# Zeroed matrix products added between the warm-up and the first real product of a decoder trunk

## The reference, cut to what matters

```python
h = rms_norm(x, norm_mix[l])
proj = h @ w_in[l]                       # 2048 x 5120
q, k, v, hq, hf, hi, hg, cb, cc, ch = jnp.split(proj, split_idx, axis=-1)
a = swa_prompt(...)  # or swa_sample: windowed attention with sinks
o, S_new = hgrn2_mixer(hq, hf, hi, hg, S0, lower_bound[l], hgrn_norm[l])
yc, buf_new = short_conv(cc * ch, buf, conv_w[l])
x = x + jnp.concatenate([a, o, cb * yc], axis=-1) @ w_out[l]
h = rms_norm(x, norm_ffn[l])
gate, up = jnp.split(h @ w_gate_up[l], 2, axis=-1)
x = x + (jax.nn.silu(gate) * up) @ w_down[l]
```

## Time and profile before

| | |
|---|---|
| median of the two runs | 2547.41 us (2547.26 to 2547.55) |
| profiled execution | 2545.56 us |
| its span, first to last instruction | 2544.0 us |
| TensorE busy | 2530.7 us, 19426 matrix instructions |
| VectorE, ScalarE, GpSimd busy | 1475.7, 1016.2, 330.8 us |
| first warm-up pass, first real product (starts) | 1.74 and 9.79 us |

### The profile page before, as it was taken

The page is one execution under the profiler, slowest core; times in us unless marked ns, Lnnn a source line. Parts: engine busy times, 40 slices in busy tenths (PEclk is TensorE's granted clock), DMA queues, the critical chain, the costliest instruction groups (busy, mean ns, idle before and its releaser), DMA issues.

```text
span 2544.0 us, 51052 instructions
## 1 busy us (share of the span) xinstructions
PE 2530.7 (99%) x19426; PEld 2503.1 (98%) x19426; DVE 1475.7 (58%) x2011; ACT 1016.2 (40%) x1412; POOL 330.8 (13%) x279
## 2 busy tenths in 40 slices
PE   9999999999999999999999999999999999999998
PEld 9999999999999999999999999999999999999998
DVE  6678787555554445555545787775555444555544
ACT  5454554333333333333334545443333333333333
POOL 3011003111110011111100200131111000111111
PEclk9999999999999999999999999999999999999999
DMA  6545445454455444454455554454444554544553
GB/s 233 173 159 182 158 143 170 157 165 165 165 171 168 157 165 165 165 165 166 165 166 166 177 174 153 142 166 166 165 165 165 165 168 163 165 165 165 166 166 136
DMA packets 116516, 420.84 MB, mean 165 GB/s; under 512 B 13840, under 2 KB 15120, under 8 KB 116368
## 3 DMA queue, kind: packets, MB, share of 16 engines
q1 hardware_dynamic: 109296, 397.72, 47.2%
q0 software_dynamic: 4112, 14.78, 1.8%
q10 hardware_dynamic: 3024, 7.16, 0.9%
HBM read 411.06 MB, written 11.87 MB: 166 GB/s over the span
## 4 chain that ended last, share of the span: by engine, by line
PE 97%; DVE 1%; ACT 1%; issue 0%; DVEq 0%; POOL 0%; POOLq 0%
PE gp L1601 31%; PE gp L1605 31%; PE gp L1603 31%; PE mb L1654 1%; PE mb L1765 0%; PE mb L1778 0%; PE mb L1847 0%; PE mb L1786 0%; PE mb L1663 0%; ACT sc L564 0%; PE mb L1712 0%; PE mb L1729 0%; ACT sc L562 0%; DVE wlo L767 0%; PE mb L1840 0%
## 5 line engine op out<-in xcount | busy, mean ns | idle before, releaser
L767 DVE TENSOR_TENSOR wlo<-raw,whi 128x1024 fp32r<-128x1024 f32 x754 | 987.0, 1343 | 362.7 <-ACT whi L427 359.3
L427 ACT ACTIVATE whi<-raw 128x1024 fp32r<-128x1024 f32 x754 | 768.7, 1051 | 583.6 <-PE gp L1605 549.5
L1601 PE MATMUL gp<-xh,whi 128*128 128x288 f32 x4096 | 885.7, 297 | 0.0
L1605 PE MATMUL gp<-xl,whi 128*128 128x288 f32 x4096 | 877.0, 295 | 0.0
L1603 PE MATMUL gp<-xh,wlo 128*128 128x288 f32 x4096 | 875.0, 295 | 0.0
L1601 PEld LDWEIGHTS gp<-xh,whi 128*128 128x128 f32 x4096 | 656.5, 188 | 7.7 <-issue 5.9
L1603 PEld LDWEIGHTS gp<-xh,wlo 128*128 128x128 f32 x4096 | 659.2, 188 | 0.0
L1605 PEld LDWEIGHTS gp<-xl,whi 128*128 128x128 f32 x4096 | 655.7, 188 | 0.0
L1605 PE MATMUL gp<-fl,whi 128*128 128x288 f32 x1408 | 303.2, 296 | 0.0
L1603 PE MATMUL gp<-fh,wlo 128*128 128x288 f32 x1408 | 301.1, 295 | 0.0
L1601 PE MATMUL gp<-fh,whi 128*128 128x288 f32 x1408 | 301.0, 294 | 0.0
(11 more groups left out here) (266 smaller groups left out, 1656.2 us busy)
## 6 DMA issues: line engine op xcount, KB each, us to landing
raw<-wstream SPq DMA_DIRECT2D x754, 512.0 KB, 4.3
s<-s_cache POOLq DMA_DIRECT2D x8, 512.0 KB, 10.6
hs_out<-s ACTq DMA_DIRECT2D x8, 512.0 KB, 3.3
caches_out<-caches POOLq DMA_DIRECT2D x8, 496.0 KB, 8.7
x<-x_in ACTq DMA_DIRECT2D x4, 576.0 KB, 8.6
kct<-kt_cache POOLq DMA_DIRECT2D x4, 512.0 KB, 6.1
vct<-v_cache POOLq DMA_DIRECT2D x4, 512.0 KB, 6.8
y_out<-x SPq DMA_DIRECT2D x3, 576.0 KB, 2.9
```

Of the source, the lines that this page charges most:

```text
L427: a.activation(whi[slot][:], raw[slot][:], ACT.Copy).then_inc(hi_ready, 1)
L767: v.tensor_tensor(wlo[slot][:], raw[slot][:], whi[slot][:].bitcast(F32), ALU.subtract).then_inc(lo_ready, 1)
L1601: t.matmul(outs[c], whi[slot][:, k, c * P:(c + 1) * P], mv_hi, start=first, stop=False)
L1605: mm = t.matmul(outs[c], whi[slot][:, k, c * P:(c + 1) * P], mv_lo, start=False, stop=end)
```

## The change

GpSimd's list of memsets becomes two longer: `zero_w`, 384 numbers per partition, and `zero_m`, 4096 numbers per partition, both zero, of type fp32r, both starting on a multiple of 512 bytes in `wide`. The waits for `ones_set` on ScalarE, VectorE and TensorE go from 5 to 7. Behind the warm-up TensorE does 22 series. A series is one product of `mean_x` with itself into `mb[1]`, and then a list of rounded products of 128 x 128 zeroed weights and 288 zeroed columns, all added up in `mb[0]`. Each product of the list names the byte at which its weights begin in `zero_w` and the byte at which its columns begin in `zero_m`.

- 11 series of ten products with the same two offsets: 0, 32, 64, 128 or 256 bytes for the one, the other or both.
- 5 series of ten in which the columns alternate between offset 0 and 1152, 1280, 1536, 8192 or 8320 bytes.
- 3 series of 24 that step through four rows of 1152, 1280 or 1536 bytes, with three products a row: the row itself, one 8192 bytes on, and the first again with weights 512 bytes on.
- 3 series of 24 with six products a row, with the weights and columns in the order of the kernel's own blocks.

```diff
+        warm = [wide[0] + (-wide[0]) % 512, wide[1]]
+        zero_w = sub(warm, "zero_w", [P, 384], F32R)
+        warm[0] = warm[0] + (-warm[0]) % 512
+        zero_m = sub(warm, "zero_m", [P, 4096], F32R)
...
-            a.wait_ge(ones_set, 5)
+            a.wait_ge(ones_set, 7)
...
-                v.wait_ge(ones_set, 5)
+                v.wait_ge(ones_set, 7)
...
+            e.memset(zero_w[:].bitcast(F32), 0.0).then_inc(ones_set, 1)
+            e.memset(zero_m[:].bitcast(F32), 0.0).then_inc(ones_set, 1)
...
-            t.wait_ge(ones_set, 5)
+            t.wait_ge(ones_set, 7)
             for _ in range(AWAKE):
                 t.matmul(mb[0][:, 0:P], mean_x[:], mean_x[:], start=True, stop=True)
+            def series(pairs):
+
+                t.matmul(mb[1][:, 0:P], mean_x[:], mean_x[:], start=True, stop=True)
+                for i, (w_at, m_at) in enumerate(pairs):
+                    t.matmul(mb[0][:, 0:TOK], zero_w[:, w_at // 4:w_at // 4 + P], zero_m[:, m_at // 4:m_at // 4 + TOK],
+                             start=(i == 0), stop=(i == len(pairs) - 1))
+
+            for w_at, m_at in ((0, 0), (64, 0), (128, 0), (256, 0), (0, 64), (0, 128), (0, 256), (64, 64), (128, 128), (0, 32), (32, 0)):
+                series([(w_at, m_at)] * 10)
+            for step in (1152, 1280, 1536, 8192, 8192 + 128):
+                series([(0, step * (i % 2)) for i in range(10)])
+            for pitch in (1152, 1280, 1536):
+                series([(512 * (j == 2), pitch * k + 8192 * (j == 1)) for k in range(4) for j in range(3)] * 2)
+            for pitch in (1152, 1280, 1536):
+                series([(512 * (j in (1, 3)), pitch * k + 8192 * (j > 3)) for k in range(4) for j in range(6)])
```

## The result

The changed kernel took 2593.89 us (median of two runs, 2593.58 to 2594.19) against 2547.41 us before: a ratio of 1.0187, 95% interval 1.0170 to 1.0204. It is 46.5 us slower, within the forecast range, 2.2 us under the forecast value. Its profiled execution took 2594.19 us with a span of 2592.6 us; the working said 2594.2 and 2592.65 us.

A forecast was written before the change was run, and what follows sets the result against it. TensorE, busy 99% of the span, was taken to bound the kernel. 3.85 + 0 + 4.9 + 40.3 - 0.4 = 48.65 us on the 2547.4 us median gave 2596.1 us, 1.91% longer, range 2592.0 to 2600.3 us.

The forecast's parts named there:

- What bounds the kernel: Whole kernel: TensorE, busy 99% of the span, is the chain; added instructions cost their own time unless it would have waited.
- Part 1: Start: TensorE waits for two more GpSimd memsets (0.42 and 3.56 us), adding 3.85 us, bounds 3.4 to 4.3 us.
- Part 2: TensorE's 46 warm-up passes: start later but keep their 8.05 us; no change, range -1.3 to +0.5 us.
- The clock in part 2: Warm-up passes: spacings of 0.213 and 0.111 us fit 1.2 and 2.4 GHz, though the granted clock's row reads 1.00 throughout.
- Parts 3 and 4: Series behind the warm-up: 22 full-precision separators cost 4.9 us, 304 zeroed products at 132.7 ns cost 40.3 us.
- (a): Zeroed products: loads no longer hide behind columns; likelier size 2600 us, worst case 2630 us; chance 0.12.
- (b): Zeroed products: no hold-up at most offsets, 0.121 us a product, 3.6 us less, 2592.5 us; chance 0.13.
- The rule weighed against the rows: Zeroed products: the skill's columns / 2.4 plus 2.5 ns gives 122.5 ns, 37.2 us in all; the trace's 132.7 ns disagrees.
- Part 5: First 240 real products: TensorE's small holes waiting for xl close, so at most 0.4 us comes back.
- The sum and the base: Whole kernel: 48.65 us of terms, added to the 2547.4 us median rather than the profiled 2545.56 us, give 2596.1 us.
- The 2% point: Whole kernel: 50.9 us slower, 2.3 us beyond the forecast; chance 0.16 of over 2% slower, 0.83 of within 2%.

The follow-up runs named there:

- the second time: The changed kernel with its 22 series run twice: 2638.15 us, against 2593.0 us for the changed kernel on the same chip.
- the memsets alone: The changed kernel without its series, keeping only the two memsets and raised waits: 2548.18 us, 2.6 us over the kernel before.
- the run without the collision: The kernel before with one more wait: GpSimd sums the first squares only after VectorE's last xl; ten of eleven runs at 2545.22 to 2545.57 us.
- the changed kernel's second profile: The changed kernel run again without edit, against the kernel before: median 2593.0 us, ratio 1.0185; profiled span 2591.7 us.
- the run with other sizes: The changed kernel with eleven series of 12 products of other sizes and types in place of its 22 series: 2573.8 us.

## Why the prediction was right, step by step

- **What bounds the kernel.** Right. The 45 us were paid in full at the start and 45.1 us more the second time; the 7.7 us put at the end, where TensorE isn't the chain, cost next to nothing.
- **Part 1, 3.85 us.** 3.82 us in the changed kernel, 3.8 us by moving the wait behind the warm-up. The line through three short memsets held at seven times their size: 3.52 us for 3.56 us. That ScalarE's and VectorE's delays cost nothing beside the series held too, though they were misread: ScalarE's table load isn't behind the wait (3.75 us, 3.71 us before), and the first xl start 1.1 us later (8.63 for 7.55 us), not 2 us.
- **Part 2, no change.** It came out for the two profiled executions (8.05 and 8.15 us), and that is luck: behind the later start the warm-up took 6.64 to 8.15 us in the traces of this study, the lower end 0.1 us outside the stated range. It was the term with the largest real scatter, and it spoiled the expectation of the memsets alone by 1.1 us. The prediction also missed that the kernel before hides a short warm-up. In the run without the collision the clock rises 3.7 us after the first pass in place of 6.1 us, yet the first real product starts at 9.54 us, just behind VectorE's first four xl, which run from 7.63 to 9.43 us. In the changed kernel the series follow at once, and the whole difference is seen at the end.
- **The clock in part 2.** The two rates are the two levels of the granted clock, as the prediction supposed. That its row reads 1.00 for the slow passes too is only for want of a record: in each of the fourteen traces the first record, of 1.00, begins where the spacing falls (7.83 us in the kernel before), and the row counts a stretch without a record as 1.00.
- **Parts 3 and 4, 4.9 + 40.3 us.** 45.09 us, against 45.2 us. With 4.9 us for the separators a product takes 132.2 ns; the forecast said 132.7. All series of ten lie within 1.53 and 1.56 us. So offsets and row lengths decide at most a few ns, rivals (a) and (b) are both out, and one bank did cost nothing.
- **The rule weighed against the rows.** The 122.5 ns worked out from the Trainium skill (TensorE: Matmul & The Clock Gate, Back-to-back issue gap) were too few for these products, as the rows of before had said, and are right for bf16 (122 ns).
- **Part 5, -0.4 us.** 0.47 us.
- **The sum and the base.** The sum is 48.65 us, the traces' shift 48.6 us; so close by the luck of part 2, since with the changed kernel's second profile the shift is 47.7 us. The 2.2 us that are missing are those of the last step, "The median of the two runs is 2547.41 us, 1.85 us above the profiled one, so I forecast 2547.4 + 48.7". I took the 1.85 us for an offset that both kernels carry. It is the collision at 18 us: the profiled execution of before didn't have it (its xl took 0.51 us), and both timed runs (2547.26 and 2547.55 us), which have no trace, lie where the long kind lies. In the changed kernel VectorE is done with xl by 19 us and TensorE comes at 58.80 us, so the collision, if it happens, isn't on the path, and the change pays back 1.7 us against a long execution of before. Had I added the sum to the profiled execution's own time, 2594.2 us, the miss would have been 0.3 us.
- **The 2% point.** It was right to see it near; measured ratios are 1.0187 and 1.0185, both intervals reaching to about 1.020.

## What to carry to other kernels

Where one engine is the chain for 99% of the span, price an addition by the start-to-start spacing of the nearest rows of the same shape on that engine, and ask of the place only whether the engine would have waited there: 50 products of one shape cost 7.7 us at the start and nothing at the end. Before adding a difference to a median, see whether the profiled execution and the timed runs are of one kind; two runs that agree to 0.3 us may both be of the kind that the profile doesn't show. When a wait is added ahead of a warm-up, put it behind the warm-up instead if the warm-up doesn't need it, which was worth 3.8 us here.

## What the runs showed of the hardware that I had not expected

- A rounded 4-byte product of 256 to 512 columns costs 11 to 16 ns more than its columns at 2.4 GHz, with 32 to 128 weight columns alike; a bf16 product costs 2 ns more.
- The stretch of slow passes at TensorE's start lasted from about 3 us (the run with other sizes, whose warm-up ends at 12.20 us) to about 6 us, in executions that are otherwise alike. The first record of the granted clock begins at its end each time; the row's 1.00 ahead of it is no reading.
- VectorE's copy of four numbers took 2.60 us in the changed kernel and ended at 5.53 us, with zero_m's memset on GpSimd, which ran from 1.99 to 5.51 us; before, the same copy took 0.17 us. In all nine traces with that memset the copy ends at 5.53 us, wherever it starts between 2.84 and 3.60 us, and in the five without it takes 0.17 us. No run moves the memset away, so that it holds the copy up is argued from these ends:

```profile
2.93 2.60 DVE L1247 COPY lbt<-par 128x4 f32<-128x4 f32 x1 [2.93 <-DMA par<-params]
```

- One VectorE instruction of 0.51 us takes 1.70 us when it loses to a GpSimd sum beside it, which here is the difference between 2545.6 and 2547.3 us for the kernel. Which of the two loses can't be told from their starts: VectorE won when it started 0.02 to 0.30 us behind GpSimd and lost when it started 0.05 to 0.27 us behind.
